# A two-layer decoder step: pairs of output tiles, their PSUM banks taken in turn, around the norms

## The reference, cut to what matters

```
x = layer_norm(DEEPNORM_ALPHA * x + merged @ w_out, ln1_g, ln1_b)
hdn = jnp.square(jax.nn.relu(x @ w_up))
x = layer_norm(DEEPNORM_ALPHA * x + hdn @ w_down, ln2_g, ln2_b)
```

## Time and profile before

| | us |
|---|---|
| median of 3 runs | 2130.46 (2130.21 to 2131.23) |
| the profiled execution | 2129.4 |
| span of its trace, first to last instruction | 2127.6 |
| TensorE busy in the span | 2106.3 (99%), 15716 matmuls |
| GpSimd, VectorE, ScalarE busy | 1311.1, 1047.9, 524.9 |

### The profile page before, as it was taken

One profiled execution on the slowest core, in us unless ns is written; L12 is line 12 of the kernel. 1 busy time (PEld: TensorE's weight loads), 2 busy tenths in 40 slices (PEclk: granted clock), 3 DMA queues, 4 the chain that ended last, 5 costly groups with the idle time before them and its releaser, 6 DMA issues.

```text
span 2127.6 us, 38066 instructions
## 1 busy us (share of the span) xinstructions
PE 2106.3 (99%) x15716; PEld 2044.7 (96%) x15716; DVE 1047.9 (49%) x1669; ACT 524.9 (25%) x935; POOL 1311.1 (62%) x1549
## 2 busy tenths in 40 slices
PE   8999999999999999999999999999999999999997
PEld 8898999999999999999998989999999999999997
DVE  6156300534278873626781571006424787726257
ACT  5121121041014141414241210210410231514133
POOL 6744558645683947466757346676456748475574
PEclk9999999999999999999999999999999999999999
DMA  5415324234231323222223153332342213222331
GB/s 178 132 52 168 127 82 139 76 107 161 95 100 60 100 80 100 80 84 80 96 72 119 59 173 110 115 120 76 113 169 84 96 60 99 80 81 79 100 100 45
DMA packets 200324, 215.41 MB, mean 101 GB/s; under 512 B 5600, under 2 KB 192992, under 8 KB 200160
## 3 DMA queue, kind: packets, MB, share of 16 engines
q1 hardware_dynamic: 170688, 172.84, 25.2%
q10 hardware_dynamic: 29472, 40.20, 5.5%
HBM read 199.06 MB, written 13.97 MB: 100 GB/s over the span
## 4 chain that ended last, share of the span: by engine, by line
PE 96%; DVE 3%; ACT 0%; ACTq 0%; issue 0%; POOL 0%; DVEq 0%
PE gp L583 53%; PE gp L1108 13%; PE gp L606 9%; PE gp L597 7%; PE qb L686 7%; PE gp L760 3%; PE qb L760 2%; PE gp L950 1%; PE gp L938 1%; PE qb L726 1%; DVE r L2158 1%; DVE x_lo L2064 0%; DVE r L2058 0%; DVE r L2055 0%; DVE m_lo L1666 0%; DVE m_hi L1665 0%
## 5 line engine op out<-in xcount | busy, mean ns | idle before, releaser
L466 POOL TENSOR_TENSOR w_lo<-stage,w_hi 128x256 fp32r<-128x256 f32 x1008 | 815.9, 840 | 90.7 <-ACT w_hi L1202 70.7
L463 POOL TENSOR_SCALAR w_hi<-stage 128x1024 fp32r<-128x1024 f32 x240 | 253.1, 1054 | 497.8 <-PE gp L583 244.5
L583 PE MATMUL gp<-b_hi,w_hi 128*128 128x288 f32 x1408 | 321.6, 295 | 0.0
L583 PE MATMUL gp<-x_hi,w_hi 128*128 128x288 f32 x1408 | 321.3, 295 | 0.0
L583 PE MATMUL gp<-b_hi,w_lo 128*128 128x288 f32 x1408 | 318.5, 293 | 0.0
L583 PE MATMUL gp<-b_lo,w_hi 128*128 128x288 f32 x1408 | 318.5, 293 | 0.0
L583 PE MATMUL gp<-x_hi,w_lo 128*128 128x288 f32 x1408 | 318.4, 293 | 0.0
L583 PE MATMUL gp<-x_lo,w_hi 128*128 128x288 f32 x1408 | 318.4, 293 | 0.0
L583 PEld LDWEIGHTS gp<-b_hi,w_hi 128*128 128x128 f32 x1408 | 231.6, 188 | 2.4 <-issue 2.2
L583 PEld LDWEIGHTS gp<-x_hi,w_hi 128*128 128x128 f32 x1408 | 231.4, 188 | 2.3 <-issue 2.1
L583 PEld LDWEIGHTS gp<-b_lo,w_hi 128*128 128x128 f32 x1408 | 231.5, 188 | 1.0 <-issue 1.0
(11 more groups left out here) (299 smaller groups left out, 4272.3 us busy)
## 6 DMA issues: line engine op xcount, KB each, us to landing
stage<-in_w_in SPq DMA_DIRECT2D x54, 1024.0 KB, 5.4
stage<-in_w_up SPq DMA_DIRECT2D x32, 1024.0 KB, 5.3
stage<-in_w_down SPq DMA_DIRECT2D x32, 1024.0 KB, 5.0
stage<-in_w_in SPq DMA_DIRECT2D x40, 256.0 KB, 4.3
stage<-in_w_ret_out SPq DMA_DIRECT2D x8, 1024.0 KB, 5.3
stage<-in_w_mem_kv SPq DMA_DIRECT2D x8, 1024.0 KB, 5.2
stage<-in_w_out SPq DMA_DIRECT2D x8, 1024.0 KB, 5.0
s_in_c<-in_ret_state ACTq DMA_DIRECT2D x8, 512.0 KB, 4.8
```

What stands on the lines that cost most here:

```text
L463: nc.gpsimd.tensor_scalar(hi, raw, 1.0, 1.0, ALU.mult, ALU.mult).then_inc(hi_done, 1)
L466: ins = nc.gpsimd.tensor_tensor(lo[:, k:k + 2, :], raw[:, k:k + 2, :], hi[:, k:k + 2, :].bitcast(F32), ALU.subtract)
L583: last = mm(gp[:, 2 * (i % 2) + half, 0:HALF], w[:, i % 4, k * P:(k + 1) * P], x(k, half), start=(k == n == 0), stop=(k == nk - 1 and n == 2))
```

## The change

`half_rows` takes a pair of tiles instead of one, and goes from one tile's bank to the other's at each matmul; the semaphore of a finished tile is counted in it. `four_a`, `four_b` and `closing_four` call it for the pairs (0, 1) and (2, 3). In `four_a` and `four_b` the first pair already shared its k-loop, with three matmuls of a tile at a time. In `closing_four` the tiles were made one by one, and the statistics of half 0 stood after half of tile 0's matmuls in half 1; now they stand after half of the matmuls of pair (0, 1). Up tile 4, the first full tile behind `four_b` in the up projection, is made with `by_half`.

```diff
-        def half_rows(j, half, hi, lo, ks):
+        def half_rows(js, half, hi, lo, ks, done=None):
             for k in ks:
                 for n, (w, x) in enumerate(((w_hi, hi), (w_hi, lo), (w_lo, hi))):
-                    last = mm(gp[:, j, 0:HALF], w[:, j, k * P:(k + 1) * P], x(k, half), start=(k == n == 0),
-                              stop=(k == KT - 1 and n == 2))
-            return last
+                    for j in js:
+                        last = mm(gp[:, j, 0:HALF], w[:, j, k * P:(k + 1) * P], x(k, half), start=(k == n == 0),
+                                  stop=(k == KT - 1 and n == 2))
+                        if k == KT - 1 and n == 2:
+                            last.then_inc(done, 1)
...
             for j in (2, 3):
                 may_start_a(l, t, j)
-                half_rows(j, 0, *X, range(KT)).then_inc(half_done, 1)
+            half_rows((2, 3), 0, *X, range(KT), half_done)
...
             for j in (2, 3):
                 pe.wait_ge(bank_free, l * 4 + j + 1)
-                half_rows(j, 1, *X, range(KT)).then_inc(tile_done, 1)
+            half_rows((2, 3), 1, *X, range(KT), tile_done)
...
         def closing_four(l, t, x, hi, lo):
 
-            for j in range(4):
-                may_start_a(l, t, j)
-                half_rows(j, 0, hi, lo, range(KT)).then_inc(half_done, 1)
-            for j in range(4):
-                pe.wait_ge(added_a, l * 8 + 4 * x + j + 1)
-                last = half_rows(j, 1, hi, lo, range(KT // 2))
-                if j == 0:
+            for js in ((0, 1), (2, 3)):
+                for j in js:
+                    may_start_a(l, t, j)
+                half_rows(js, 0, hi, lo, range(KT), half_done)
+            for js in ((0, 1), (2, 3)):
+                for j in js:
+                    pe.wait_ge(added_a, l * 8 + 4 * x + j + 1)
+                half_rows(js, 1, hi, lo, range(KT // 2))
+                if js[0] == 0:
                     norm_stats(l, x, 0)
-                last = half_rows(j, 1, hi, lo, range(KT // 2, KT))
-                last.then_inc(tile_done, 1)
+                half_rows(js, 1, hi, lo, range(KT // 2, KT), tile_done)
...
-                        product(l, T_FF + i, (T_FF + i) // 2, i, *X)
+                        product(l, T_FF + i, (T_FF + i) // 2, i, *X, by_half=(i == 4))
```

More of the change, by code:

```diff
@@ L621, in four_a @@
                         pe.wait_ge(x_ready[0], k + 1)
[L622 to L625, removed]
+                        half_rows((2 * two, 2 * two + 1), 0, *X, [k], half_done)
                 return
@@ L630, in four_a @@
                 pe.wait_ge(x_ready[0], x_count(l, t) + k + 1)
[L631 to L634, removed]
+                half_rows((0, 1), 0, *X, [k], half_done)
                 if k == KT // 2 - 1:
@@ L646, in four_b @@
                 pe.wait_ge(x_ready[1], x_count(l, t) + k + 1)
-                for j in range(2):
-                    last = half_rows(j, 1, *X, [k])
-                    if k == KT - 1:
-                        last.then_inc(tile_done, 1)
+                half_rows((0, 1), 1, *X, [k], tile_done)
             for j in (2, 3):
                 pe.wait_ge(bank_free, l * 4 + j + 1)
-                half_rows(j, 1, *X, range(KT)).then_inc(tile_done, 1)
+            half_rows((2, 3), 1, *X, range(KT), tile_done)
         def x_count(l, t):
```

## The result

The changed kernel takes 2155.72 us (median of 4 runs, 2152.93 to 2157.63), beside 2130.34 us for the kernel before (4 runs, 2129.14 to 2131.23): a ratio of 1.0119, 95% interval 1.0106 to 1.0131. It is slower, as forecast, by 25.4 us and not by 12.7, and lies above the range.

The account below looks back on a forecast made before the run. TensorE's matmuls one after another plus its standstills bound the kernel. Terms 9.6 + 2.0 + 0.9 + 0.2 = 12.7 us on the profiled 2129.4 give 2142.1, plus 1.1 to the median: 2143.2 us, range 2137 to 2148.

Parts of the forecast that it names:

- Pairs in `closing_four`, half 1: Tiles closing later in half 1 of `closing_four` delay `four_a`'s operands: 3.2 us at each of three norms, +9.6 us.
- The restart: `four_a`'s start behind three norms: TensorE waits for late slot 1, then late `x_lo`, +9.6 us in all.
- VectorE's chain decides, weights are just inside it: Start of `four_a`: slot 1 lets TensorE reach the fourth k-tile at 668.5, before its `x_lo` at 669.4; cost 3.2 us.
- Rival 4: Clock falls in the new waits before `four_a`, adding 2.4 to 5.1 us: 2145.6 to 2148.3 us, chance 0.10.
- The waits of `four_b`: `four_a`'s pair (2, 3) delays `x_lo` for `four_b`: 0.4 us twice, 1.2 us in layer 1's q/k projection, together +2.0 us.
- The pace of the pairs: Matmuls alternating two tiles of one half: pace taken as unchanged, 0 us; bounds -3.8 to +1.2 us.
- Rivals 1 and 2: Paired matmuls: alternation reaches 130.0 ns, 2139.4 us, chance 0.25; or pace below 124.2 ns makes the kernel faster, chance 0.04.
- Rival 5: Cycling through banks makes the clock go up and down: 1536 matmuls at 240 ns, +165 us, 2308 us, chance 0.01.
- The products behind: Products after the first four tiles: 192 behind the q/k four may change between 130.0 and 133.3 ns, 0.6 us either way.
- Tile 4's own 0.12 us: Up tile 4 bank by bank: 48 matmuls at 132.5 instead of 130.0 ns, twice, +0.2 us.
- The end: After the last `closing_four`, tile 2's later add pushes the square of the mean from 2115.14 to 2116.05, +0.9 us.

Follow-up runs that it names:

- experiment 2: Changed kernel with half 0 of `closing_four` tile by tile, half 1 still in pairs: 2145.75 us, ratio 1.0078.
- experiment 3: Changed kernel with half 1 of `closing_four` tile by tile, its statistics where they stood before, half 0 still in pairs: 2141.02 us, ratio 1.0050.
- experiment 4: Two kernels: changed kernel, `closing_four` half 0 tile by tile, half 1 pairing only (0, 1), 2145.48 us, or only (2, 3), 2144.86 us.
- experiment 5: Changed kernel with overwritten filler matmuls in the long waits, 22 ahead of `four_a`'s second slot, 24 ahead of the closing pair's: 2151.95 us.
- Experiment 8: Changed kernel with `closing_four` and `four_a`'s tiles 2 and 3 tile by tile, up tile 4 still bank by bank: 2134.01 us, ratio 1.0019.
- experiment 9: Changed kernel with `closing_four` and `four_a`'s tiles 2 and 3 tile by tile, up tile 4 by halves in turn: 2130.27 us, ratio 0.9999.
- experiment 1: Changed kernel with `closing_four` tile by tile in both halves, the rest of the change kept: 2132.55 us, ratio 1.0014.
- experiment 6: Changed kernel without `by_half` in up tile 4, its halves in turn as before: 2154.69 us, ratio 1.0114.
- experiment 11: Kernel before with one extra 288-column matmul ahead of up tile 4 in both layers, nothing else changed: 2133.96 us, ratio 1.0019.

## Why the prediction was wrong

- **The step that failed is "Pairs in `closing_four`, half 1".** It costed the end of the pairs, who waits for tiles that close late, and stopped there. The same edit's half 0 has a beginning: a pair asks for both weight slots before its first matmul. The forecast asked that of `four_a` (slot 1) but not of the pair (2, 3) in half 0, which stands in its sum with nothing. Two waits of 2.84 and 2.83 us followed, 9.0 us with the matmuls at the lower clock behind them. Experiments 2 and 3 set this apart from the restarts.
- **The restart was right in mechanism and near in size**: 10.8 us for 9.6. Slot 1 and `x_lo` both come late, by the routes described, and experiment 4 shows each alone. "VectorE's chain decides, weights are just inside it" held only at full clock (experiment 5); in the changed kernel the weights' wait came first and the slow matmuls behind it used up the rest.
- **Rival 4 came true in kind**, with 0.10 given to it: the clock fell in the waits. Its time did not (2145.6 to 2148.3), for the closings of norm 1 are not in it. Its own price was put at 2.4 to 5.1 us for three restarts, and the three restarts exceed their waits by 0.93 + 0.71 + 0.68 = 2.3. Taking the long waits' idleness away gave back 3.8 us over all five places, some 1.5 of it at the restarts. The earlier trace rows had shown 15 slow matmuls after the start's wait, and that row deserved more than 0.10. The Trainium skill, "TensorE: Matmul & The Clock Gate", section "HAM oscillation — how this bites in real kernels", describes waits for operands between bursts of matmuls that put the clock back to its lower level; the traces here agree, with 10 to 14 matmuls at 240 ns behind 15 of the 18 waits of 2.6 to 2.8 us, and only the first one drawn out behind waits of 0.72 to 1.09. The same page's "Back-to-back issue gap" gives columns / 1.2 ns when cold, 240 ns for 288 columns, which is what the rows show.
- **The waits of `four_b`**: 0.4, 1.2 and 0.4 us were forecast, 0.34, 1.29 and 0.35 measured. Experiment 8 removes them by undoing the one pair named.
- **The pace of the pairs** was taken as unchanged, and is: half 0 at 131.8 and 132.0 ns (norm 0, layers 0 and 1; before 131.7), half 1 at 133.3. Rivals 1 and 2 fall, and experiment 9 shows it for the pairs of `four_b` with nothing else in the way. Rival 5 falls too: the clock is full through all pairs except behind a wait.
- **The products behind** were let off at 0.2 us in sum, with 0.6 us either way for 192 others. The earlier trace rows showed two paces for the same kind of stream, and the forecast bounded the pairs by them but not the products that follow: 576 matmuls at 133.3 instead of 130.0 in each layer are 2 x 1.9 us, here 3.8. Tile 4's own 0.12 us in each layer was right (experiment 1).
- **The end** cost 0.5 us for 0.9: set against TensorE's last matmul, the square of the mean came 0.7 us later, and VectorE's operation behind it 0.55.

What stays open is what sets the pace. Of the kernels with tile 4 bank by bank, experiments 1 and 2 had the fast pace in both layers and experiment 3 in one; the others were slow in both. With tile 4 as before, the kernel before and experiment 9 were fast, and experiment 6 slow. No run here says what in the stream tells them apart. Each of these paces is that of one traced execution; the traced one of experiment 2 was the fastest of its four by 1.9 us, so the others may have run at the slow pace, which no trace shows.

## What to carry to other kernels

When tiles are paired, cost both ends of the pair: it closes its first tile later, and it opens its second tile earlier. At every place where the pair stands, compare when each operand of the second tile was ready with when it will be asked for; 0.38 us in hand against 3.2 us asked was in two rows of the trace. A wait of nearly 3 us on TensorE costs its length and, behind most such waits here, the slow matmuls that follow, so shorten it first. And a difference of 3 to 4 us between two versions may be the pace of a long stream that neither of them touches: look at the spacing of the matmuls behind an edit before crediting the edit.

## What the hardware showed that was not expected

A stream of alternating 288-column matmuls at the upper clock level holds one of two paces for hundreds of matmuls: 128 and 132 ns in turn (130.0), or 131, 131, 131, 140 (133.3). A single matmul ahead of it moved it from the first to the second, 1.9 us in each layer (experiment 11). Behind waits of 2.6 to 2.8 us the clock fell 15 times and stayed up three times (experiment 4). Two operands that are each about 3 us late for the same start cost 10.4 us over three restarts, where each alone cost 9.7 and 8.2.
